# A hybrid attention layer: the output weight split in its own landing place, w_in halves in landing order, modulation waves cut into parts

## The reference

```
shift, scale, gate = split(silu(c) @ w_ada + b_ada)          # w_ada 1024 x 3072
h = rmsnorm(x, g_pre) * (1 + scale) + shift
q, k, v, gg, ga, sq, sk, sv, sg = split(h @ w_in)            # w_in 1024 x 2832
gla = rmsnorm_per_head(gated_linear_attention(q, k, v, log_sigmoid(ga @ w_alpha + b_alpha) / 16)) * silu(gg)
swa = sliding_window_attention(rope(sq), rope(sk), sv, window 128, with sinks) * silu(sg)
y = x + gate * rmsnorm(concat(gla, swa) @ w_out, g_post)     # w_out 1024 x 1024
```

## Time and profile before

| | |
|---|---|
| median of 3 runs (lowest, highest) | 1600.25 us (1598.66, 1600.52) |
| profiled execution | 1596.66 us |
| its span, first to last instruction | 1594.9 us |
| TensorE busy | 1522.9 us, 95% of the span |
| VectorE busy | 1020.0 us, 64% |
| ScalarE busy | 594.4 us, 37% |
| granted TensorE clock, mean | 0.982 of 2.4 GHz |

### The profile page before, as it was taken

How to read it: one execution, slowest core, us unless ns; L and a number is a source line. 1 busy time by engine, 2 the same in 40 slices (tenths; PEclk the granted TensorE clock), 3 DMA queues, 4 the chain that set the end, 5 groups by cost and what they waited for, 6 DMA issues and landing times.

```text
span 1594.9 us, 30628 instructions
## 1 busy us (share of the span) xinstructions
PE 1522.9 (95%) x11968; PEld 895.0 (56%) x11968; DVE 1020.0 (64%) x1746; ACT 594.4 (37%) x1814; POOL 361.4 (23%) x478
## 2 busy tenths in 40 slices
PE   4697999999999999999999999999999999999994
PEld 2363655665555656665555656656556656655552
DVE  1886566666676666667666666767766666666752
ACT  2633334333343334334343333333333343333331
POOL 1121222222222222212222222212222222223121
PEclk9898999999999999999999999999999999999997
DMA  9863433233333333233333332333333332343222
GB/s 316 269 185 90 90 90 80 65 85 77 61 83 82 89 89 73 70 88 76 63 77 88 89 89 63 78 89 76 63 76 89 89 86 63 81 80 79 38 63 56
DMA packets 306795, 144.97 MB, mean 91 GB/s; under 512 B 268177, under 2 KB 293226, under 8 KB 306762
## 3 DMA queue, kind: packets, MB, share of 16 engines
q1 hardware_dynamic: 306176, 144.31, 37.3%
q10 hardware_dynamic: 586, 0.21, 0.1%
HBM read 63.14 MB, written 17.56 MB: 51 GB/s over the span
## 4 chain that ended last, share of the span: by engine, by line
PE 91%; DVE 3%; SPq 2%; DMA 2%; issue 1%; ACT 0%; POOL 0%; ACTq 0%; DVEq 0%
PE bank L435 58%; PE pairP L435 22%; PE pairQ L530 2%; PE pairQ L606 2%; PE pairQ L534 2%; PE pairQ L562 2%; PE pairQ L570 1%; SPq L300 1%; DMA w_lo<-in_w_ada 1%; PE bank L583 1%; DVE w_lo L929 1%; PE bank L616 1%; DVE wo_lo L925 0%; PE bank L612 0%; DVE etmp L1110 0%
## 5 line engine op out<-in xcount | busy, mean ns | idle before, releaser
L435 PE MATMUL bank<-w_hi,hT 128*128 128x512 f16 (+1 forms) x2640 | 738.5, 360 | 8.6 <-DVE w_lo L929 8.6
L435 PE MATMUL bank<-w_lo,hT 128*128 128x512 f16 (+1 forms) x1320 | 474.7, 360 | 0.0
L435 PEld LDWEIGHTS bank<-w_hi,hT 128*128 128x128 f16 x2640 | 258.4, 98 | 265.9 <-issue 14.6
L435 PE MATMUL pairP<-wo_hi,late 128*128 128x512 f16 x1056 | 321.5, 381 | 12.2 <-DVE wo_lo L925 11.1
L435 PE MATMUL pairP<-wo_lo,late 128*128 128x512 f16 x528 | 201.1, 381 | 0.0
L435 PEld LDWEIGHTS bank<-w_lo,hT 128*128 128x128 f16 x1320 | 129.3, 98 | 118.8 <-issue 0.8
L435 PE MATMUL bank<-hT,w_hi 128*128 128x128 f16 x2112 | 183.4, 221 | 10.1 <-DVE w_lo L929 6.8
L435 PE MATMUL bank<-hT,w_lo 128*128 128x128 f16 x1056 | 181.2, 221 | 0.0
L435 PEld LDWEIGHTS pairP<-wo_hi,late 128*128 128x128 f16 x1056 | 103.8, 98 | 137.8 <-issue 13.4
L435 PEld LDWEIGHTS bank<-hT,w_hi 128*128 128x128 f16 x2112 | 165.4, 99 | 18.2 <-issue 7.1
L1018 DVE SCALAR_TENSOR_TENSOR gates<-pairQ,o_r,gates 128x128 f32<-128x128 f32 x132 | 37.2, 346 | 149.1 <-ACT o_r L687 149.1
(11 more groups left out here) (202 smaller groups left out, 2101.0 us busy)
## 6 DMA issues: line engine op xcount, KB each, us to landing
x_in<-in_x_prompt SPq DMA_DIRECT2D x32, 512.0 KB, 3.5
x_res<-in_x_prompt SPq DMA_DIRECT2D x32, 512.0 KB, 3.9
out<-stage SPq DMA_DIRECT2D x32, 512.0 KB, 2.9
wo_lo<-in_w_in SPq DMA_DIRECT2D x6, 1024.0 KB, 7.2
w_hi<-in_w_ada SPq DMA_DIRECT2D x4, 1024.0 KB, 9.2
w_lo<-in_w_ada SPq DMA_DIRECT2D x4, 1024.0 KB, 12.8
wo_hi<-in_w_in SPq DMA_DIRECT2D x3, 1024.0 KB, 10.6
late<-pair_tok SPq DMA_TRANSPOSE x165, 3.2
```

Of the source, the lines that this page charges most:

```text
L435: last = pe.matmul(out, a(c, i), b(c, j), start=(c == 0 and n == 0), stop=(c == KC - 1 and n == 2))
```

## The change

Three edits, and what moves with them.

The w_out halves share one tensor `wo` of 16 rows of 1024 f16. A w_out row block of float32 fills two of its rows (`out_rows`), the low half is written over the first of them, and the high half goes into rows that have been used up (`WO_HI`, `WO_LO`). All eight blocks are loaded by one `load_out`, at the end of step 0, and split two by two in step 1.

w_in units 10 and 11 and the four gate units get other slots; the first gate unit is loaded ahead of `turn_heads`. In step 0 the halves of units 6 to 11 and h of tile 1 stand in another order, and q/k waits for one unit at a time.

Waves 1 and 2 are multiplied in parts: units 0 and 1, then 2, then 3 in wave 1; units 0 to 2, then 3 in wave 2.

```diff
-UNITS += [("in", i, slot) for i, slot in enumerate((3, 4, 5, 6, 2, 1, 3, 4, 5, 6, 3, 4))]
-UNITS += [("ada", GATE_UNIT + i, slot) for i, slot in enumerate((5, 6, 3, 4))]
-UNITS += [("out", i, slot) for i, slot in enumerate((18, 19, 20, 18, 19, 18, 19, 18))]
+UNITS += [("in", i, slot) for i, slot in enumerate((3, 4, 5, 6, 2, 1, 3, 4, 5, 6, 1, 3))]
+UNITS += [("ada", GATE_UNIT + i, slot) for i, slot in enumerate((4, 5, 6, 3))]
+WO_LO = [2 * i + 2 for i in range(OUT_UNITS - 1)] + [2 * OUT_UNITS - 1]
+WO_HI = [0, 1] + [2 * i - 1 for i in range(2, OUT_UNITS)]
...
-        wo_hi = sb("wo_hi", [P, KC, D], F16)
-        wo_lo = sb("wo_lo", [P, KC, D], F16)
+        wo = sb("wo", [P, 2 * OUT_UNITS, D], F16)
...
+        out_rows = [wo[:, 2 * i + 2:2 * i + 4, :].rearrange("p c n -> p (c n)").bitcast(F32)
+                    for i in range(OUT_UNITS - 1)] + [stage[:, 2 * D:3 * D]]
...
+            def load_out():
+                sp.wait_ge(sem["mod_mm"], 3)
+                sp.wait_ge(w_split, len(IN_UNITS))
+                for i in range(GH):
+                    sp.dma_start(out_rows[i], w_out[0, i * P:(i + 1) * P, :]).then_inc(out_loaded[i // 2], 16)
+                for i in range(GH, OUT_UNITS):
...
+                        sp.dma_start(out_rows[i][HD * pp:HD * (pp + 1), :], w_out[0, row:row + HD, :])\
+                          .then_inc(out_loaded[i // 2], 16)
...
                 if c.first:
                     turn_h(c)
-                    sp.wait_ge(w_split, split_number("out", 2) + 1)
+                    load_out()
                 if c.cur:
                     turn_probs(c)
...
-                held = [unit_number("ada", 4 * wave + j) for j in range(4)]
-                for n in held:
-                    pe.wait_ge(staged[UNITS[n][2]], 16 * (slot_use(n) + 1))
-                for c in range(KC):
-                    for j, n in enumerate(held):
...
+                for together in ((0, 1, 2, 3),) if wave == 0 else ((0, 1, 2), (3,)) if wave == 2 else ((0, 1), (2,), (3,)):
+                    held = [(j, unit_number("ada", 4 * wave + j)) for j in together]
+                    for j, n in held:
+                        pe.wait_ge(staged[UNITS[n][2]], 16 * (slot_use(n) + 1))
+                    for c in range(KC):
+                        for j, n in held:
...
-                        pe.wait_ge(w_split, in_units_before[W_QK])
...
                     for b in range(4):
+                        if c.first and b % 2 == 0:
+                            pe.wait_ge(w_split, b // 2 + 1)
...
+                    if kind == "out":
+                        if i == 0:
+                            act.wait_ge(sem["mod_mm"], 3)
+                        else:
+                            act.wait_ge(w_split, len(IN_UNITS) + max(i - 1, 0))
+                        act.wait_ge(out_loaded[i // 2], 32 if i < GH else 64)
+                        act.activation(wo[:, WO_HI[i], :], out_rows[i], ACT.Copy, scale=WSCALE).then_inc(w_half, 1)
+                        continue
```

More of the change, by code:

```diff
@@ L251, in hybrid_layer @@
             sem[name] = ctx.enter_context(nc.semaphore(name))
+        out_loaded = [ctx.enter_context(nc.semaphore(f"out_loaded{i}")) for i in range(OUT_UNITS // 2)]
         staged = {slot: ctx.enter_context(nc.semaphore(f"staged{slot}")) for slot in sorted({u[2] for u in UNITS})}
@@ L288, in load_unit @@
                 kind, i, slot = UNITS[n]
-                before = [u for u in UNITS[:n] if u[2] in SAME_PLACE.get(slot, (slot,))]
+                before = [u for u in UNITS[:n] if u[2] == slot]
                 if before and before[-1][0] == "ada":
@@ L295, in load_unit @@
                     src, w = w_ada[0, :, i * UNIT:(i + 1) * UNIT], UNIT
-                elif kind == "in":
+                else:
                     src, w = w_in[0, :, IN_UNITS[i][1]:IN_UNITS[i][1] + IN_UNITS[i][2]], IN_UNITS[i][2]
[L298 to L303, removed]
+                dst = slots[slot][:, 0:KC * w].rearrange("p (c n) -> p c n", c=KC)
+                sp.dma_start(dst, src.rearrange("(c p) n -> p c n", p=P)).then_inc(staged[slot], 16)
+            def load_out():
[4 more added lines that the diff above has]
+                for i in range(GH, OUT_UNITS):
                     g, e = (i - GH) // 2, (i - GH) % 2
@@ L368, in program @@
                           .then_inc(sem["res_copied"], 16)
-                if c.second:
-                    load_out((3, 4))
                 if c.next and c.prev and not c.last:
                     turn_h(c)
+                if c.first:
+                    load_unit(unit_number("ada", GATE_UNIT))
                 if c.cur:
@@ L375, in program @@
                 if c.first:
-                    for i in range(GATE_UNIT, ADA_UNITS):
+                    for i in range(GATE_UNIT + 1, ADA_UNITS):
                         load_unit(unit_number("ada", i))
-                    load_out((0, 1, 2))
                 if c.last or c.sample:
@@ L795, in program @@
                         h_tok_hi(c)
+                    if c.second:
+                        split_hi([("out", 0), ("out", 1)])
                     act.wait_ge(sem["sq_mm"], t + 1)
@@ L851, in program @@
                     act.activation(etmp[:, :], bank6[:, :], ACT.Exp, scale=-DESCALE).then_inc(sem["gg_e"], 1)
-                    if c.second:
-                        split_hi([("out", 7)])
                     act.wait_ge(sem["sg_mm"], t + 1)
@@ L877, in program @@
                     act.activation(pair_tok[:, 0, :], late[:, 0:D], ACT.Copy).then_inc(sem["p_hi"], 1)
-                    if c.first:
-                        split_hi([("out", 0), ("out", 1), ("out", 2)])
                 if c.after:
@@ L1030, in program @@
                 if c.second:
+                    split_lo([("out", 0), ("out", 1)])
+                if c.second:
                     dve.wait_ge(sem["cache_lo"], 1)
@@ L1063, in program @@
                     if c.first:
-                        make_h(c)
-                        split_lo([("in", 8)])
+                        split_lo([("in", 9)])
+                    if c.second:
+                        split_lo([("out", 4), ("out", 5)])
                     dve.wait_ge(sem["z_l"], t + 1)
@@ L1113, in program @@
                        .then_inc(sem["gg_x"], 1)
-                    if c.second:
-                        split_lo([("out", 7)])
                     dve.wait_ge(sem["sc_mm"], t + 1)
@@ L1172, in program @@
                     dve.reciprocal(rden[:, :], den[:, :]).then_inc(sem["rden"], 1)
-                    if c.first:
-                        split_lo([("out", 0), ("out", 1), ("out", 2)])
                 if c.sample:
```

62 lines of the change are left out of this document (26 added, 36 removed).

## The result

The changed kernel takes **1590.05 us** (median of five runs, 1587.1 to 1590.55) against 1599.75 us before (five runs, 1597.56 to 1600.52). The ratio is 0.9942 with a 95% interval of 0.9931 to 0.9954: 0.6% faster, some 9.5 us. Forecast were 1587.5 us and a gain of 12.7.

A forecast was written before the change was run, and what follows sets the result against it. TensorE bounds the kernel, so prologue gains arrive whole. Wave two -0.6, tile 0 +7.6, wave three -3.4, tile 1's h +4.9, new wait -9.3, output wait +11.1, output clock +2.4: 12.7 sooner, 1587.5 us; range 1578 to 1598.

The forecast's parts named there:

- Wave two: Second modulation wave: three passes of 3.43 us, 10.3 in all at full clock, ending at 37.9, 0.6 us later.
- rivals 2 and 3: Clock falls in wave two's single passes, 1589.5 to 1593.5 (20%); all five passes of both waves at 1.2 GHz, 1604 (8%).
- Wave three: Third modulation wave: two passes, 6.9 us plus a 0.2 us tail, giving back 3.4 us of tile 0's gain.
- Tile 0: Tile 0's products: reordered weight splits gain 7.6 us inside it, mostly at the gate product; last matmuls end at 84.0.
- The new wait: Tile 1, TensorE waits 7.3 us for row steps behind transposes queued after output rows; with its low clock, -9.3 us.
- The bound named for this, 110: Latest landing of tile 0's probability transposes, if twelve smaller transfers stream a fifth slower; 108.0 was forecast.
- The output wait and its clock: Before tile 1's output product the 11.1 us weight wait goes; the product at full clock gains 2.4 us.
- Rival 4: Output weight halves stay late in tile 1, the old wait partly returns: 1597 to 1600 us, 10%.
- rival 1: Probability transposes not held up by output rows: about 1 us idle in tile 1, no clock loss, 1580 us, 17%.

The follow-up runs named there:

- a4: Changed kernel with the second modulation wave's four units multiplied as one pass again, once the last has landed: 1589.56 us, ratio 0.9942 to the kernel before.
- a3: Changed kernel with the third modulation wave's four units multiplied as one pass again: 1585.09 us, ratio 0.9915 to the kernel before.
- c3: Changed kernel with the third modulation wave in four passes of one unit each instead of two passes: 1593.66 us, ratio 0.9967 to the kernel before.
- c1: Changed kernel with VectorE's low half of w_in unit 9 moved back behind tile 0's decay chain: 1591.07 us, ratio 0.9963 to the kernel before.
- c2: Changed kernel with VectorE's low half of w_in unit 8 moved behind GpSimd's rotary steps: 1586.21 us, ratio 0.9928 to the kernel before.
- b2: Changed kernel with the twelve output-row transfers issued on ScalarE's queue instead of SyncE's: 1587.94 us, ratio 0.9941 to the kernel before.
- a1: Changed kernel with SyncE issuing tile 0's two probability transposes ahead of the twelve output-row transfers: 1582.57 us, ratio 0.9903 to the kernel before.

## Why the prediction was right, and what it mis-sized

The kernel is faster by the mechanism forecast: one large wait goes, a smaller one of another kind comes, and nothing is given back in tiles 2 to 31. The lead of the profiled execution over the one before, at points along the path (one execution each, so good to about 1 us up to wave three by the spread above):

| at | forecast | measured |
|---|---|---|
| tile 0's last matmuls end | 7.0 | 5.0 |
| wave three ends | 3.6 | 2.4 |
| tile 1's first product starts | 6.9 | 5.7 |
| tile 1 is through sq | 8.5 | 7.1 |
| the step behind the new wait starts | 1.3 | -2.2 |
| tile 1's output product starts | 10.4 | 7.2 |
| it ends | 12.7 | 9.6 |

- **Wave two: the sign was wrong, the size small.** Three passes were priced at 10.3 us; they took 8.89, because a pass starts beside the last rounds of the one before. The row for it was there: two units' records stand beside each other in the earlier trace rows, and nothing said that this stops where a pass ends. The clock stayed at 1.00 (all records 379 to 403 ns), so rivals 2 and 3 fall. The levels that the recorded texts call 2.4 and 1.2 GHz are the profile's 1.00 and 0.50; it prints no GHz, and what it shows is 128x512 matmuls that start every 0.216 us at 1.00 (before, 305.68 to 310.43 us), some 2.4 columns a ns. The wave gave a lead of 1.6 us where -0.6 was forecast, but 0.6 of it is that this execution came to the wave at 26.82 instead of 27.41, and the times show no worth of the edit (a4).
- **Wave three: -3.4 forecast, -2.6 measured**, by the same overlap (a3 and c3).
- **Tile 0: 7.6 forecast for its inside, 3.4 measured.** From wave two's end to tile 0's last matmul it is 53.7 us before and 50.4 after. The largest miss of the sum is here, and that the table shows only 2.0 of it is luck: wave two's 2.2 stand against it. The order of the splits did most of what was said: the gate product started at 70.98, forecast 70.15, though TensorE was there 1.6 us sooner than forecast, and c1 puts unit 9's place alone at about 3.4 us. I missed that unit 8's split, moved forward, lies beside the rotary steps on GpSimd and holds one for 2 us (c2), and with it, behind the rotary steps, unit 9's high half on ScalarE; and the low clock lasted longer: the product's first 6.0 us ran at a mean of 0.52, an estimated 5.8 us of them at the low level, where the 7.44 us of before at 0.71 make some 4.3.
- **The new wait: -9.3 forecast, -11.4 measured** (9.5 us, and 3.9 us at half clock). Its chain was right to 0.2 us: 5.4 us from landing to row step, 5.55 forecast. The mis-sized step is "1.04 MB more stand ahead: 14.3 + 2.6 = 16.9 us": all of the rows were priced at the 398 GB/s of the earlier trace rows, which was read while rows of 128 partitions were moving, and half of them go at 219 to 242. The rate for that shape was in the trace of before, 238 GB/s from 135 to 138 us (shown above), and was left unused. From the first row's issue (92.36) to the landing it took 19.4 us. At 230 GB/s half the rows cost an estimated 3.9 us more than at 398, and the whole came out 2.5 longer, so some other part was priced too long; which, no run shows. The bound named for this, 110, was too near as well. That the transposes "are issued behind them on SP's queue" gave the right order for a wrong reason: b2 has nearly the same landing (110.3) from two queues.
- **The output wait and its clock: right.** No wait before the product, which ran 10.50 us at 1.00; the last low half was done by 138.7, 1.8 us before it. Rival 4 falls with that, rival 1 with the landing at 111.76. No run puts the output rows back into their old places, so the 11.1 us are read from the two traces alone.

Of the 3.1 us missing at the end of tile 1, 1.4 are missing before the new wait (4.2 in tile 0 and 0.2 in tile 1's start, less 2.2 in wave two and 0.8 in wave three), 2.1 come with the wait, and 0.4 are given back.

## What to carry to other kernels

In these runs a bulk load ahead of small transfers delayed them, from whatever queue it started: with 4.19 MB of rows ahead the probabilities' transposes landed at 111.8 us, with the rows on another queue at 110.3, with 2.1 MB ahead at 102.5. Issue such a load in parts between them, and read the rate from rows of the same shape (up to 420 GB/s for 128 partitions, 219 to 242 for 64). When a wait is taken away, look up what each later transfer or step would wait for, and put first on each engine what the longest path needs. Price an added pass by what it overlaps with (2.6 us here, not 3.43), and check what a step that is moved now lies beside (2.40 us instead of 0.35).

## What the hardware showed unexpectedly

- The passes of a wave, whose units write different 32 rows of the result, overlapped by about four rounds where one followed the other: 2.6 us for each further pass of 16 rounds, not 3.43 (3.66, 6.27, 11.50 us for one, two and four).
- Loads in pieces of 256 KB into 64 partitions: 219 to 242 GB/s; of 512 KB into 128: up to 420 (a1, 100 to 102 us). A load whose source had an outer dimension of 2: 53 GB/s at a DMA share of 0.13.
- A GpSimd step of 0.35 us took 2.40 beside a VectorE split.
- The clock's last low stretch differs between executions of the same code there, 2.6 us in all.
